# Sampled attention: where the last gate weights are loaded, when GpSimd works on the linear branch, and where queries are spread and first keys turned

## What is computed

```
h  = modulate(rmsnorm(x), c)
qa, ka, va, ra, lra, qb, kb, vb, fb, ga, gb = split(h @ w_in)
o_a = gated linear attention (4 heads), normalised, times silu(ra)
o_b = forgetting attention (8 heads of 128):
      prompt:  softmax(q k^T * scale + F_t - F_s), causal, with the prompt's own keys
      sample:  the same over 1024 past positions, fetched by page_table from
               cache_k / cache_v in pages of 128, and over the 4 new tokens
x += gt1 * ((sigmoid(ga) * (o_a @ w_up_a) + sigmoid(gb) * (o_b @ w_up_b)) @ w_out)
x += gt2 * mixture of 16 experts (top 2 of one group)(modulate(rmsnorm(x), c))
```

## Time and profile before

| | us |
|---|---|
| runs shown (3) | 1968.68, 1970.84, 1976.9; median 1970.84 |
| the profiled execution, its own time | 1969.51 |
| its span, first to last instruction | 1967.7 |
| TensorE busy in the span | 1776.0 |
| clock granted to TensorE, mean over the span | 0.954 of full |

### The profile page before, as it was taken

How to read it: one execution, slowest core, us unless ns; L and a number is a source line. 1 busy time by engine, 2 the same in 40 slices (tenths; PEclk the granted TensorE clock), 3 DMA queues, 4 the chain that set the end, 5 groups by cost and what they waited for, 6 DMA issues and landing times.

```text
span 1967.7 us, 28092 instructions
## 1 busy us (share of the span) xinstructions
PE 1776.0 (90%) x11120; PEld 1113.9 (57%) x11120; DVE 532.4 (27%) x1146; ACT 209.5 (11%) x403; POOL 158.5 (8%) x274
## 2 busy tenths in 40 slices
PE   6579999999998999996888999998699898899998
PEld 3046666666566787775666777775333333333335
DVE  2020000000008664436554111113323322231233
ACT  2010000000001110211222110002200001000002
POOL 1011011110201000240000000000100000000000
PEclk9889999999998999998998999998799999998999
DMA  9998766685714433556999884424299999999992
GB/s 356 422 355 295 254 256 243 221 320 201 276 67 141 146 98 109 196 194 214 392 393 347 331 318 141 132 90 167 75 383 398 408 384 385 398 405 383 406 391 99
DMA packets 150458, 530.86 MB, mean 270 GB/s; under 512 B 17701, under 2 KB 61899, under 8 KB 123611
## 3 DMA queue, kind: packets, MB, share of 16 engines
q1 hardware_dynamic: 124980, 432.32, 57.8%
q0 software_dynamic: 17088, 97.15, 14.1%
q10 hardware_dynamic: 8336, 0.66, 0.3%
HBM read 510.94 MB, written 19.15 MB: 269 GB/s over the span
## 4 chain that ended last, share of the span: by engine, by line
PE 74%; DMA 13%; DVE 5%; issue 3%; SPq 3%; DVEq 1%; ACT 1%; POOLq 0%; POOL 0%; ACTq 0%
PE ps L632 71%; DMA ring<-in_w_up_e_dram 4%; DMA xT<-in_w_ada_dram 3%; DMA ring<-in_w_ada_dram 3%; PE ps L642 2%; DMA xT<-in_w_in_dram 2%; SPq L384 1%; SPq L378 1%; DVE z L1399 1%; DVE ring L1396 1%; DVE z L1390 1%; DMA z<-in_x_sample_dram 0%; DVE ring L1746 0%; DVEq L2024 0%; DVE ring L1486 0%
## 5 line engine op out<-in xcount | busy, mean ns | idle before, releaser
L632 PE MATMUL ps<-hT,ring 128*128 128x288 f32 x2304 | 586.6, 412 | 9.9 <-ACT hT L1212 6.5
L632 PEld LDWEIGHTS ps<-hT,ring 128*128 128x128 f32 x2304 | 433.5, 191 | 168.0 <-issue 55.1
L632 PE MATMUL ps<-ring,work 128*64 128x512 f32 (+1 forms) x1280 | 277.3, 631 | 39.6 <-DMA ring<-in_w_ada_dram 26.4
L632 PE MATMUL ps<-z,ring 128*128 128x288 f32 (+1 forms) x1040 | 255.5, 407 | 4.5 <-PE ps L632 2.8
L1399 DVE COPY z<-ps 128x256 f32<-128x256 f32 (+7 forms) x98 | 64.3, 660 | 689.8 <-PE ps L632 668.7
L632 PE MATMUL ps<-ring,z 32*32 32x256 f32 (+3 forms) x3744 | 217.2, 400 | 23.2 <-DVE z L1399 11.1
L632 PEld LDWEIGHTS ps<-z,ring 128*128 128x128 f32 x1040 | 196.4, 190 | 62.8 <-issue 7.6
L632 PEld LDWEIGHTS ps<-ring,work 128*64 128x64 f32 (+1 forms) x1280 | 77.5, 135 | 205.9 <-issue 165.6
L632 PEld LDWEIGHTS ps<-ring,z 32*32 32x32 f32 (+3 forms) x3744 | 108.9, 114 | 120.1 <-issue 113.0
L1212 ACT ACTIVATE z<-ps 128x512 f32<-128x512 f32 (+4 forms) x108 | 60.4, 601 | 921.4 <-PE ps L632 908.3
L1396 DVE SCALAR_TENSOR_TENSOR xT<-ps,modT,xT 128x256 f32<-128x256 f32 x160 | 70.8, 480 | 252.8 <-PE ps L632 252.7
(11 more groups left out here) (203 smaller groups left out, 806.2 us busy)
## 6 DMA issues: line engine op xcount, KB each, us to landing
ring<-in_w_in_dram SPq DMA_DIRECT2D x36, 2048.0 KB, 12.8
xT<-in_w_ada_dram POOLq DMA_DIRECT2D x64, 1024.0 KB, 7.1
ring<-in_w_gate_e_dram SPq DMA_DIRECT2D x32, 2048.0 KB, 13.1
ring<-in_w_up_e_dram SPq DMA_DIRECT2D x32, 2048.0 KB, 18.4
ring<-in_w_down_e_dram SPq DMA_DIRECT2D x32, 2048.0 KB, 14.9
ring<-in_w_ada_dram SPq DMA_DIRECT2D x16, 2048.0 KB, 26.2
ring<-in_cache_v_dram SPq DMA_DIRECT2D x64, 512.0 KB, 5.8
ring<-in_cache_k_dram SPq DMA_DIRECT2D x64, 512.0 KB, 5.9
```

Of the source, the lines that this page charges most:

```text
L632: return nc.tensor.matmul(o, lhsT, rhs, start=start, stop=stop, skip_group_check=free)
```

## The change

- The last gate load (m = 11) goes to slot 5 instead of slot 1, and has a semaphore of its own, `last_gates_full`. SP issues it after a wait for `oa_final`.
- SP's order after load m = 10 becomes: value pages into slots 2 and 3, store 18 and 19, key pages of sequence 0 into slot 1, wait for `oa_final`, the last gate load, store 20 and 21, key pages into slot 0, store 22 and 23, key pages of sequence 1 into slots 0 and 1.
- GpSimd does its work on `oaT` first, and issues the six stores of new keys and values behind it.
- VectorE raises `f_ready` before it copies `vbTok`; TensorE waits for the values in front of the first product with them instead of in front of the loop.
- The spreading of `q4` moves into rounds 5 and 6 of the prompt's loop on VectorE, 8 copies each, behind a wait for the six stores. Its first two transposes of keys move into rounds 7 and 8: the slot 1 pages in round 7, the slot 0 pages in round 8, each in front of all of that round's other VectorE work.
- Of sequence 0, VectorE turns n = 2 and 3 behind a wait for gate tile 24, since they go to slot 5.

```diff
--- before.py
+++ after.py
@@ -61,7 +61,7 @@
...
         "gla_sample_ready os_turned_copied ms_a_ready rs_a_ready rs_a_inverted "
-        "kv_tok_ready gla_scratch_free f_ready s_new_copied ob_ready work_free ms2_ready logits_copied member_ready pos_ready "
+        "f_ready kv_tok_ready gla_scratch_free s_new_copied ob_ready work_free ms2_ready logits_copied member_ready pos_ready "
         "table_ready list_ready").split(),
...
@@ -282,7 +282,7 @@
...
 
-            later = LATER if n >= UP and n % SLOTS < 2 else 0
+            later = LATER - n % SLOTS if n >= UP and n % SLOTS < 2 else 0
             return n // SLOTS - (1 if n % SLOTS < 2 else 0) + later
...
@@ -306,7 +306,7 @@
...
 
-            return place(UP + m % 2) - LATER + m // 2
+            return place(UP + m % 2) - (LATER - m % 2) + m // 2
 
...
@@ -358,14 +358,17 @@
...
 
-            for m in range(12):
+            def gate_columns(m):
+                at = (COL_GA, COL_GB)[m // 8] + m % 8 * 256
+                return io["w_in"][0, :, at:at + 256].rearrange("(k p) n -> p k n", p=P)
+
+            for m in range(11):
                 sp.wait_ge(sem(f"ring_free{m % 2}"), later_place(m) + 1)
-                at = (COL_GA, COL_GB)[m // 8] + m % 8 * 256
-                sp.dma_start(slot(m % 2).rearrange("p (k n) -> p k n", k=KT),
-                             io["w_in"][0, :, at:at + 256].rearrange("(k p) n -> p k n", p=P)).then_inc(sem(f"ring_full{m % 2}"), 16)
+                sp.dma_start(slot(m % 2).rearrange("p (k n) -> p k n", k=KT), gate_columns(m)).then_inc(sem(f"ring_full{m % 2}"), 16)
                 if m >= 2:
...
                     store_gate(2 * m - 3)
+
             def gates_back(g):
...
@@ -392,12 +395,16 @@
...
             pages(0, 3, lead(3))
+            store_gate(18)
+            store_gate(19)
+            pages(0, 1)
+            sp.wait_ge(sem("oa_final"), 1)
+            sp.dma_start(slot(5).rearrange("p (k n) -> p k n", k=KT), gate_columns(11)).then_inc(sem("last_gates_full"), 16)
             store_gate(20)
...
             store_gate(23)
-            pages(0, 1)
             pages(1, 0)
...
@@ -561,14 +568,6 @@
...
             pool.tensor_tensor(sig8, ra, sig8, ALU.mult).then_inc(sem("gate_a_ready"), 1)
-            pool.wait_ge(*step("kv_tok_ready"))
-            pool.dma_start(out["k_prompt"][0, 0].rearrange("(c p) h d -> p c (h d)", p=P), kbTok).then_inc(sem("kv_stored"), 16)
-            pool.dma_start(out["v_prompt"][0, 0].rearrange("(c p) h d -> p c (h d)", p=P), vbTok).then_inc(sem("kv_stored"), 16)
-            pool.dma_start(out["k_sample"][0].rearrange("b t h d -> (b t) (h d)"), kbS).then_inc(sem("kv_stored"), 16)
-            pool.dma_start(out["v_sample"][0].rearrange("b t h d -> (b t) (h d)"), vbS).then_inc(sem("kv_stored"), 16)
-            pool.dma_start(out["logf_prompt"][0, 0].rearrange("(c p) h -> p c h", p=P), lfTok[:, 0:2, :]).then_inc(sem("kv_stored"), 16)
-            pool.dma_start(out["logf_sample"][0].rearrange("b t h -> (b t) h"), lfTok[0:TS, 2, :]).then_inc(sem("kv_stored"), 16)
-
             pool.wait_ge(*step("rs_a_inverted"))
...
@@ -578,6 +577,14 @@
...
             pool.sem_inc(sem("oa_final"), 1)
+            pool.wait_ge(*step("kv_tok_ready"))
+            pool.dma_start(out["k_prompt"][0, 0].rearrange("(c p) h d -> p c (h d)", p=P), kbTok).then_inc(sem("kv_stored"), 16)
+            pool.dma_start(out["v_prompt"][0, 0].rearrange("(c p) h d -> p c (h d)", p=P), vbTok).then_inc(sem("kv_stored"), 16)
+            pool.dma_start(out["k_sample"][0].rearrange("b t h d -> (b t) (h d)"), kbS).then_inc(sem("kv_stored"), 16)
+            pool.dma_start(out["v_sample"][0].rearrange("b t h d -> (b t) (h d)"), vbS).then_inc(sem("kv_stored"), 16)
+            pool.dma_start(out["logf_prompt"][0, 0].rearrange("(c p) h -> p c h", p=P), lfTok[:, 0:2, :]).then_inc(sem("kv_stored"), 16)
+            pool.dma_start(out["logf_sample"][0].rearrange("b t h -> (b t) h"), lfTok[0:TS, 2, :]).then_inc(sem("kv_stored"), 16)
+
             pool.wait_ge(sem("state_stored"), 48)
...
@@ -746,16 +753,18 @@
...
                     if k == 0:
-                        if j % 2 == 0:
+                        if j == 22:
+                            pe.wait_ge(sem("last_gates_full"), 16)
+                        elif j % 2 == 0:
                             pe.wait_ge(sem(f"ring_full{m % 2}"), 16 * (later_place(m) + 1))
...
                             pe.wait_ge(sem("gate_copied"), j - 1)
-                    w = slot(m % 2).rearrange("p (k n) -> p k n", k=KT)[:, k, j % 2 * P:(j % 2 + 1) * P]
+                    w = slot(m % 2 if m < 11 else 5).rearrange("p (k n) -> p k n", k=KT)[:, k, j % 2 * P:(j % 2 + 1) * P]
                     last = mm(ps[:, 7 - j % 2, 0:T], w, hT[:, k, :], k == 0, k == KT - 1)
...
                         last.then_inc(sem("gate_tile"), 1)
-                        if j % 2 == 1:
+                        if j % 2 == 1 and m < 11:
                             release("gate_tile", j + 1, m % 2)
...
@@ -900,7 +909,6 @@
...
             pe.wait_ge(*step("f_ready"))
-            pe.wait_ge(sem("tok_copied"), 4)
             for i in range(H_B + 1):
...
@@ -928,6 +936,8 @@
...
                         pe.wait_ge(sem("fox_out"), h - 1)
+                    if h == 0:
+                        pe.wait_ge(sem("tok_copied"), 4)
                     o = ps[:, 4 + h % 2, 0:TP]
...
@@ -1004,7 +1014,7 @@
...
 
-            pe.wait_ge(sem("q4_ready"), 1)
+            pe.wait_ge(sem("q4_ready"), 2)
             for half in range(2):
...
@@ -1682,28 +1692,50 @@
...
             copy(vbS.rearrange("p (a n) -> p a n", a=2), ps[0:TS, 4:6, :])
-            copy(vbTok, vtmp)
             v.wait_ge(*step("lf_turned"))
...
             copy(lfTok[0:TS, 2, :], ps[0:TS, 1, 16:24])
+            nc.vector.tensor_tensor_scan(nfT[:, 0:TP], ones[0:H_B, 0:1].to_broadcast([H_B, TP]), fT[:, 0:TP], 0.0, ALU.mult, ALU.add)
+            f4 = fT[:, TP:T].rearrange("p (b t) -> p b t", t=DT)
+            for t in range(1, DT):
+                tt(f4[:, :, t], f4[:, :, t - 1], f4[:, :, t], ALU.add)
+                v.drain()
+            copy(fT[:, 0:TP], nfT[:, 0:TP])
+            v.drain()
+            tsc(nfT[:, :], fT[:, :], -1.0, None, ALU.mult)
+            v.drain()
+            v.sem_inc(reach("f_ready"), 1)
+            copy(vbTok, vtmp)
             v.drain()
...
 
-            nc.vector.tensor_tensor_scan(nfT[:, 0:TP], ones[0:H_B, 0:1].to_broadcast([H_B, TP]), fT[:, 0:TP], 0.0, ALU.mult, ALU.add)
-            f4 = fT[:, TP:T].rearrange("p (b t) -> p b t", t=DT)
-            for t in range(1, DT):
-                tt(f4[:, :, t], f4[:, :, t - 1], f4[:, :, t], ALU.add)
-                v.drain()
-            copy(fT[:, 0:TP], nfT[:, 0:TP])
-            v.drain()
-            tsc(nfT[:, :], fT[:, :], -1.0, None, ALU.mult)
-            v.drain()
-            v.sem_inc(reach("f_ready"), 1)
+            def spread_queries(*parts):
+
+                for part in parts:
+                    for a in range(4):
+                        last = copy(q4[32 * a:32 * a + 32, :, part, :], qb[32 * part:32 * part + 32, :, TP:T])
+                last.then_inc(sem("q4_ready"), 1)
+
+            def first_keys(half):
+
+                v.wait_ge(sem(f"kv_full{half}"), 64)
+                nc.vector.transpose(kT[:, 0, 4 * half:4 * half + 4], slot(half).rearrange("p (n g e) -> p n g e", n=4, g=2)[:, :, 0]).then_inc(sem("keys_turned"), 1)
+
             for i in range(H_B + 1):
+                if i == 5:
+                    v.wait_ge(sem("kv_stored"), 6 * 16)
+                    spread_queries(0, 1)
+                if i == 6:
+                    spread_queries(2, 3)
+                if i == 7:
+                    v.wait_ge(sem("oa_final"), 1)
+                    first_keys(1)
+                if i == 8:
+                    first_keys(0)
                 if i < H_B:
...
@@ -1734,7 +1766,6 @@
...
 
-            v.wait_ge(sem("kv_stored"), 6 * 16)
             def turn_keys(b, first=0, last=4, again=True):
...
@@ -1748,21 +1779,14 @@
...
 
-            v.wait_ge(sem("oa_final"), 1)
-            turn_keys(0, 0, 1, False)
+            nc.vector.memset(o_all, 0.0)
             v.wait_ge(*step("s_new_ready"))
...
                new_mask[:, :].unsqueeze(1).to_broadcast([P, 2, TS]), ALU.add)
-            nc.vector.memset(o_all, 0.0)
             v.drain()
...
             v.sem_inc(reach("s_new_copied"), 1)
-
-            for part in range(4):
-                for a in range(4):
-                    last = copy(q4[32 * a:32 * a + 32, :, part, :], qb[32 * part:32 * part + 32, :, TP:T])
-            last.then_inc(sem("q4_ready"), 1)
 
...
@@ -1793,7 +1817,8 @@
...
 
-            turn_keys(0, 1, 4, False)
+            v.wait_ge(sem("gate_tile"), 24)
+            turn_keys(0, 2, 4, False)
             for g in range(2):
...
```

More of the change, by code:

```diff
@@ L1705, in _ @@
             v.sem_inc(reach("f_ready"), 1)
-            for i in range(H_B + 1):
+            copy(vbTok, vtmp)
```

(10 more changed lines are left out.)

## The result

The change made the kernel slower: 1988.36 us median of 11 runs against 1974.44 us median of 11 runs of the kernel before on the same chip, ratio 1.0065, 95% interval 1.0047 to 1.0083, or +12.8 us (9.3 to 16.4). The forecast was 1974.6 us against a median of 1970.84, so +3.8 us, and a range to 1980.5.

What follows compares the result with a forecast made beforehand. TensorE is busy 90%; what counts is when the DMA-saturated stretch starts, at transpose n = 2. Terms -7.6 + 2.3 + 6.8 + 2.3 = +3.8 us on the median 1970.84 give 1974.6 us, range 1964.0 to 1980.5.

Steps and rivals of the forecast that it cites:

- head start: Before the first score: keys and queries ready early let transpose n = 2 start at 894.8, 7.6 us earlier.
- round 8: Last loop round: the inserted key transpose stands in front of normalising head 7 and costs its full 2.3 us.
- stand: Round 3: TensorE needs the last gate load at 856.00, it lands at 862.8, so TensorE idles 6.8 us.
- clock: Behind TensorE's idle time in round 3: work at 1.2 GHz costs another 2.3 us, 0 if the idle is short.
- part 4: In front of the loop: f_ready comes 1.2 us earlier, but TensorE is at gate blocks until 830.2; worth nothing.
- Part 3: GpSimd's oaT work first: oa_final at about 832.4 instead of 861.8, nobody waits for it; stores have 17 us of cover.
- The first and second parts: Early keys and queries gain 7.6 us; insertions in rounds 5 to 8 cost 2.3: 5.3 us gained if gates are in time.
- Rival B: Round 3: SP's queue served first, gate load lands at 854.5, the whole 5.3 us stay, 1965.5 us; chance 0.27.
- E: Sample stretch follows TensorE, whose first score ran at 1.2 GHz; higher clock adds up to 2 us gain; chance 0.04.
- Rival D: Round 3: weights in 1 KB pieces move slower, 371 GB/s, idle of 9.8 us, +6.8 us, 1977.6 us; chance 0.05.
- Rival C: Round 3: queues mix badly at 333 GB/s, gate load lands 869.5, idle 13.5 us, +10.5, 1981.3 us; chance 0.06.
- The likeliest case: Late gate load in round 3 outweighs the gain: n = 2 starts at 906.2, +3.8 us, 1974.6 us; chance 0.58.

Runs made afterwards that it cites:

- e1_split: The kernel after with GpSimd's last product of 2304 columns cut into eight of 288 columns; ratio 1.0036 to the kernel before.
- e7_two_inputs: The kernel after with VectorE's 8x288 negation written as one instruction with two SBUF inputs instead of one; one run, 1993.35 us.

## Why the prediction was wrong

The sum had the terms head start, round 8, stand, clock. Measured in the kernel after, as differences of distances from the reciprocal:

| term | forecast | measured |
|---|---|---|
| head start from early keys and queries | -7.6 | -8.3 |
| round 8's transpose | +2.3 | +2.2 |
| stand for the gate load | +6.8 | +7.75 |
| clock behind that stand | +2.3 | about +1.7 |
| f_ready late, and the clock behind it | 0 | +6.2 |
| sum | +3.8 | +9.6 |

The head start is what the distance from head 7's turn of probabilities to n = 2 lost: 902.43 - 887.71 = 14.7 us before, 915.14 - 908.75 = 6.4 after. The 6.2 us are what round 3's turn of probabilities is late: 864.95 - 806.07 = 58.9 us against 52.7 before. They are the stand of 3.04 us, and a first round at mostly 1.2 GHz.

**The step that failed is part 4**, which put the move of f_ready at "worth nothing": it came 3.7 us later by distance (30.4 against 26.7), not 1.2 us earlier, and cost 6.2 us. Part 3 prepared this. Its "Nobody waits for oa_final itself" held, but it asked only who waits for that semaphore, not what runs beside the product in front of it. Both moves were timed rightly to within 1 us, one by one: the last product from 827.4 to 832.4 and f_ready at about 828.4 in the numbers of before. The two were never laid over each other. The cover that part 4's numbers leave for f_ready is 1.8 us of TensorE's gate blocks (828.4 to 830.2); 4.7 us of waiting went through it, and the stand is the 3.04 us. The first and second parts, the insertions in rounds 5 to 7 and the stores' cover came out as forecast. The value pages left at 838.18, 5.1 us later than in the kernel before by distance, which the prediction itself had named as a sign of being wrong.

**The stand was right in kind; that it was nearly right in size in the kernel after was luck.** The gate load landed 67.1 us behind the reciprocal instead of 59.8, 7.3 late, of which 3.4 went with the negation (63.8 in e1_split), and TensorE came for it 6.2 us late. Without the meeting (e1_split) the stand is 10.94 us, not 6.8: the pages left 1.2 us later than reckoned, and from the first page to the landing 35.5 us passed instead of 32.8. So without the meeting the change would have cost 6.2 us (105.7 against 99.4), not 3.8: in the sum the stand was 4.1 us too short, the head start about 0.8 too small and the clock about 0.6 too dear.

Where the 2.7 us of DMA time lie can be read from the rates, first in the kernel before around its undisturbed gate load, then in e1_split (start and end, length, TensorE busy, granted clock, DMA share, GB/s):

```profile
806.00:812.00 6.00, 6.00 (x34) 1.00 1.07 353
```

```profile
835.00:839.00 4.00, 4.00 (x17) 1.00 0.64 212
839.00:845.00 6.00, 6.00 (x29) 1.00 0.91 306
845.00:863.00 18.00, 14.27 (x70) 1.00 1.03 411
864.00:869.00 5.00, 0.00 (x0) 0.50 1.09 347
```

The 409 GB/s of the forecast held in the middle, 411. The gate load by itself moves slower with the DMA engines as busy, 347 to 353 GB/s; for its 2.1 MB that is 0.9 us more than at 409, an estimate from these rows. The rest lies in the first 10 us, where the engines were not yet full; GpSimd's stores start 4.6 us behind the first page there.

Rival B (in time, 1965.5 us) found nothing for it, and neither did E: the first score took 11.28 us against 11.36 before. Rival D's mechanism, pieces of weights that move slower than the mixture, is there in part, and its 32.6 us plus 3.2 are what e1_split took (35.5), but it had the slower rate over all bytes. Rival C's +10.5 us would have come near the measured +9.6 by the wrong cause: it has 13.5 us of standing in round 3 and nothing in front of the loop. The likeliest case had the right sign but less than a third of the size. The range ended 8 us short of the time, which fell where the prediction saw a chance of 0.07.

## What to carry to other kernels

When work moves on GpSimd, list which VectorE instructions will now run beside each long GpSimd instruction, and whether they read and write SBUF only; such a one can wait until GpSimd's is done, however small it is. Here a tensor_scalar and a two-input instruction did, and a reciprocal did not. Cut a long GpSimd product into pieces, or put it behind the short VectorE chain: the pieces took away all but 0.5 us of 9.9 here, and with the other two mends in place both ways gave the same stretch, 90.6 us. A load that is moved forward in one queue pushes another back: order the queue by when each is needed (the gate load in round 3, the value pages only in the sample stretch), since that alone was worth 7.5 us.

## What was not expected of the hardware

The wait was for GpSimd's whole instruction, in three kernels ending within 0.31 us of its end: 4.99, 4.98 and 5.14 us beside products of 5.12, 5.10 and 5.13 us. It held with one SBUF input and with two. The trace books the wait as length of the small instruction, not as idle time in front of it.

The low clock lasted differently behind like stands. Behind 7.75 us of idle in the kernel after it was back soon (0.92 on average from 875 to 884), behind 7.65 us in e7_two_inputs TensorE was held at 1.2 GHz for at least 10.5 us of work, and that run's stretch is 6.3 us longer, 4.6 of it between the landing of the gate load and head 7's turn of probabilities (40.1 us against 35.5). In rows:

```profile
875.00:884.00 9.00, 9.00 (x46) 0.92 0.07 24
```

```profile
872.50:883.00 10.50, 10.44 (x27) 0.50 0.00 0
```

In the kernel before the same work took 31.7 us, and 33.9 with the 2.2 us of round 8's transpose, so the low clock cost about 1.6 us in one execution and 6.2 in the other. That part of a stand's price isn't fixed by the trace of one execution; what sets it stays open here.
